# The experts' down products of a mixture-of-experts layer, all in passes of split operands, and their eviction on one engine

## The reference

```
for c in range(N_EXPERTS // EXPERT_CHUNK):
    g = einsum('td,edf->tef', xt, w_gate[sl])     # d = 1024, f = 256
    u = einsum('td,edf->tef', xt, w_up[sl])
    hdn = silu(g) * u * combine[:, sl, None]
    y = y + einsum('tef,efd->td', hdn, w_down[sl])
```

## Time and profile before

| | |
|---|---|
| median of 3 runs | 1458.14 us (1452.44 to 1460.0) |
| the profiled execution's own time | 1457.38 us |
| its span, first to last instruction | 1455.5 us |
| TensorE's granted clock, mean over the span; in the loop | 0.978; 1.00 |
| busy share of TensorE, VectorE, ScalarE, GpSimd | 94%, 68%, 47%, 31% |
| the loop over experts | about 785 to 1429 us |
| scatter `acc_dram<-arena` on the chain that ended last | 37% of the span |

### The profile page before, as it was taken

One profiled execution on the slowest core, in us unless ns is written; L12 is line 12 of the kernel. 1 busy time (PEld: TensorE's weight loads), 2 busy tenths in 40 slices (PEclk: granted clock), 3 DMA queues, 4 the chain that ended last, 5 costly groups with the idle time before them and its releaser, 6 DMA issues.

```text
span 1455.5 us, 19599 instructions
## 1 busy us (share of the span) xinstructions
PE 1372.3 (94%) x6615; PEld 983.9 (68%) x6615; DVE 988.4 (68%) x1415; ACT 687.0 (47%) x990; POOL 457.8 (31%) x384
## 2 busy tenths in 40 slices
PE   6989898999799999999999999999999999999990
PEld 5867677676688888885545666666666666666660
DVE  7997968785611111557635888888788888878765
ACT  4234554547422222310023766666666766766640
POOL 0422524333544444100010343332333322323322
PEclk8999999999999999999999999999999999999995
DMA  9044252535233333643057999999999999999954
GB/s 255 1 131 74 73 73 74 80 65 102 60 109 100 94 93 103 256 176 126 1 190 309 323 371 355 368 361 367 368 372 370 370 367 372 369 363 369 370 168 130
DMA packets 140775, 315.82 MB, mean 217 GB/s; under 512 B 18112, under 2 KB 99696, under 8 KB 115312
## 3 DMA queue, kind: packets, MB, share of 16 engines
q1 hardware_dynamic: 126384, 281.50, 55.6%
q0 software_dynamic: 14336, 33.59, 9.7%
HBM read 297.27 MB, written 34.54 MB: 228 GB/s over the span
## 4 chain that ended last, share of the span: by engine, by line
DMA 38%; PE 32%; DVE 12%; issue 8%; DVEq 4%; POOL 3%; POOLq 2%; ACT 1%
DMA acc_dram<-arena 37%; PE bank L728 8%; PE bank L730 8%; PE bank L729 8%; DVE arena L1418 6%; DVEq L1415 4%; PE bank L964 2%; PE bank L984 1%; DVE arena L1421 1%; POOL arena L675 1%; DVE arena L1696 1%; POOLq L634 1%; POOL arena L635 1%; PE bank L1058 1%; PE bank L735 1%
## 5 line engine op out<-in xcount | busy, mean ns | idle before, releaser
L1418 DVE TENSOR_TENSOR gate_up_low<-gate_up,gate_up_high 128x1024 fp32r<-128x1024 f32 x256 | 296.5, 1221 | 46.8 <-ACT gate_up_high L1164 46.3
L1164 ACT ACTIVATE arena<-bank 96x512 f32<-96x512 f32 (+5 forms) x244 | 128.8, 552 | 328.9 <-PE bank L730 129.0
L1164 ACT ACTIVATE gate_up_high<-gate_up 128x1024 fp32r<-128x1024 f32 x256 | 249.4, 1051 | 17.6 <-DMA gate_up<-moe_w_up_in 17.6
L1418 DVE TENSOR_TENSOR arena<-arena 128x512 f32<-128x512 f32 (+12 forms) x296 | 218.6, 771 | 16.9 <-ACT arena L1164 3.2
L728 PE MATMUL bank<-gate_up_high,rows_high 128*96 128x512 f32 x512 | 206.0, 402 | 4.4 <-DVE rows_low L1418 4.2
L730 PE MATMUL bank<-gate_up_high,rows_low 128*96 128x512 f32 x512 | 202.6, 396 | 0.0
L729 PE MATMUL bank<-gate_up_low,rows_high 128*96 128x512 f32 x512 | 200.9, 392 | 0.0
L735 PEld LDWEIGHTS bank<-arena 96*128 96x128 f32 (+5 forms) x1001 | 126.9, 187 | 54.4 <-issue 37.6
L595 POOL TENSOR_TENSOR wb_low<-arena,wb_high 128x1024 fp32r<-128x1024 f32 (+1 forms) x40 | 110.1, 2754 | 144.5 <-ACT wb_high L1164 144.5
L735 PE MATMUL bank<-arena 96*128 96x96 f32 (+5 forms) x1001 | 126.9, 265 | 8.5 <-DMA arena<-x_in 4.7
L1099 PE MATMUL bank<-down,arena 128*96 128x512 f32 x256 | 130.6, 592 | 0.0
(11 more groups left out here) (173 smaller groups left out, 2653.3 us busy)
## 6 DMA issues: line engine op xcount, KB each, us to landing
gate_up<-moe_w_gate_in SPq DMA_DIRECT2D x64, 1024.0 KB
gate_up<-moe_w_up_in SPq DMA_DIRECT2D x64, 1024.0 KB
down<-moe_w_down_in SPq DMA_DIRECT2D x64, 1024.0 KB
arena<-w_in_in SPq DMA_DIRECT2D x40, 512.0 KB, 4.1
arena<-w_glu_in SPq DMA_DIRECT2D x16, 512.0 KB, 4.0
arena<-w_lru_out_in SPq DMA_DIRECT2D x8, 768.0 KB, 4.7
arena<-x_in SPq DMA_DIRECT2D x8, 512.0 KB, 5.1
wu<-w_in_in SPq DMA_DIRECT2D x8, 512.0 KB, 6.6
```

The source lines that it names most:

```text
L1164: return nc.scalar.activation(out_, in_, func, **kw)
L1418: return V_.tensor_tensor(out_, a, b_, op)
```

## The change

Both halves of the down contraction are split: `down_high` and `down_low` are two operations each, `hid_high` and `hid_low` take both halves of hidden in one operation each, and `down` is 12 passes without a plain float32 matmul. ScalarE evicts both output halves, one after the other; VectorE's `y_kept` and its copy of the second half of hidden are gone, and so is the semaphore `y_e_dve`. The high parts of the down weights are now two buffers of twice the size, both on the shared expert's rows, so that expert 0's `down_high` waits for the stores.

```
-        heT = [at(b1 + 10240 + 512 * n, SL) for n in range(2)]
-        heT_hi = [part(f"hidden_high{n}", b1 + 10336 + 512 * n, 1, SL)[:, 0] for n in range(2)]
-        heT_lo = [part(f"hidden_low{n}", b1 + 10432 + 512 * n, 1, SL)[:, 0] for n in range(2)]
-        dn_hi = [part(f"down_high{n}", o, 1, D)[:, 0] for n, o in enumerate((sg_off + 4 * D, m_off))]
-        dn_lo = [part(f"down_low{n}", o, 1, D)[:, 0] for n, o in enumerate(dn_at)]
+        heT_hi = [part(f"hidden_high{n}", b1 + 10240 + 512 * n, 2, SL) for n in range(2)]
+        heT_lo = [part(f"hidden_low{n}", b1 + 10432 + 512 * n, 2, SL) for n in range(2)]
+        dn_hi = [part(f"down_high{n}", o, 2, D) for n, o in enumerate((m_off, m_off + 2 * D))]
+        dn_lo = [part(f"down_low{n}", o, 2, D) for n, o in enumerate(dn_at)]
...
             def add_expert(i, u):
                 pool.wait_ge(S["y_e_act"], 4 * i + u + 1)
-                pool.wait_ge(S["y_e_dve"], 4 * i + u + 1)
...
             def down(i, u):
                 pe.wait_ge(s_wdn[u % 4], 16 * i + 16 * (u // 4 + 1))
-                pe.wait_ge(S["dn_e_low"], 4 * i + u + 1)
+                pe.wait_ge(S["dn_e_low"], 8 * i + 2 * u + 2)
                 pe.wait_ge(S["hT_e_kept"], 4 * i + u + 1)
                 wait(pe, S["y_e_act"], 4 * i + u)
-                wait(pe, S["y_e_dve"], 4 * i + u)
                 for hf in range(2):
                     hs = slice(hf * 512, (hf + 1) * 512)
-                    mm3(banks[5 + hf][0:SL, :], heT_hi[u % 2], heT_lo[u % 2], dn_hi[u % 2][:, hs], dn_lo[u % 4][:, hs], True, False)
-                    last = mm(banks[5 + hf][0:SL, :], heT[u % 2], dn[u % 4][:, 1, hs], start=False, stop=True)
+                    for k in range(2):
+                        last = mm3(banks[5 + hf][0:SL, :], heT_hi[u % 2][:, k], heT_lo[u % 2][:, k],
+                                   dn_hi[u % 2][:, k, hs], dn_lo[u % 4][:, k, hs], k == 0, k == 1)
...
             def down_high(i, u):
                 act.wait_ge(s_wdn[u % 4], 16 * i + 16 * (u // 4 + 1))
                 wait(act, S["y_e_put"], 4 * i + u - 1)
-                if isinstance(i, int) and i == 0 and u == 1:
+                if isinstance(i, int) and i == 0 and u == 0:
                     act.wait_ge(S["acc_stored"], 16 * TT)
-                f(dn_hi[u % 2], dn[u % 4][:, 0], ACT.Copy).then_inc(S["dn_e_high"], 1)
+                for k in range(2):
+                    f(dn_hi[u % 2][:, k], dn[u % 4][:, k], ACT.Copy).then_inc(S["dn_e_high"], 1)

             def hid_high(i, u):
                 act.wait_ge(S["hT_e_put"], 4 * i + u + 1)
-                f(heT_hi[u % 2], banks[4][:, 0:SL], ACT.Copy).then_inc(S["hT_e_high"], 1)
+                f(heT_hi[u % 2], banks[4][:, 0:2 * SL].rearrange("p (k s) -> p k s", k=2), ACT.Copy).then_inc(S["hT_e_high"], 1)

             def y_kept(i, u):
                 wait(act, S["rows_added"], 64 * i + 16 * (u - 1))
                 act.wait_ge(S["y_e_put"], 4 * i + u + 1)
-                f(yb[u % 2][:, 0:512], banks[5][0:SL, :], ACT.Copy).then_inc(S["y_e_act"], 1)
+                f(yb[u % 2][:, 0:512], banks[5][0:SL, :], ACT.Copy)
+                f(yb[u % 2][:, 512:1024], banks[6][0:SL, :], ACT.Copy).then_inc(S["y_e_act"], 1)
...
-            def y_kept(i, u):
-                wait(dve, S["rows_added"], 64 * i + 16 * (u - 1))
-                dve.wait_ge(S["y_e_put"], 4 * i + u + 1)
-                V_.tensor_copy(yb[u % 2][:, 512:1024], banks[6][0:SL, :]).then_inc(S["y_e_dve"], 1)
...
-                dve.wait_ge(S["dn_e_high"], 4 * i + u + 1)
-                tt(dn_lo[u % 4], dn[u % 4][:, 0], dn_hi[u % 2].bitcast(f32), ALU.subtract).then_inc(S["dn_e_low"], 1)
-                if not isinstance(i, int) or u >= 1:
-                    y_kept(i, u - 1)
+                for k in range(2):
+                    dve.wait_ge(S["dn_e_high"], 8 * i + 2 * u + k + 1)
+                    tt(dn_lo[u % 4][:, k], dn[u % 4][:, k], dn_hi[u % 2][:, k].bitcast(f32), ALU.subtract).then_inc(S["dn_e_low"], 1)
                 wait(dve, S["y_e_put"], 4 * i + u - 1)
                 dve.wait_ge(S["hT_e_high"], 4 * i + u + 1)
-                V_.tensor_copy(heT[u % 2], banks[4][:, SL:2 * SL])
-                tt(heT_lo[u % 2], banks[4][:, 0:SL], heT_hi[u % 2].bitcast(f32), ALU.subtract).then_inc(S["hT_e_kept"], 1)
+                tt(heT_lo[u % 2], banks[4][:, 0:2 * SL].rearrange("p (k s) -> p k s", k=2), heT_hi[u % 2].bitcast(f32),
+                   ALU.subtract).then_inc(S["hT_e_kept"], 1)
```

More of the change, by code:

```diff
@@ L339, in decoder_layer @@
             sh_put sh_silu sh_hid sh_hT_put sh_hT sh_y_put sh_done texp_ready
-            xT_e_put xT_e_high xT_e_low g_e_put silu_e hid_e hT_e_put hT_e_kept y_e_put y_e_act y_e_dve
+            xT_e_put xT_e_high xT_e_low g_e_put silu_e hid_e hT_e_put hT_e_kept y_e_put y_e_act
              hT_e_high dn_e_high dn_e_low
@@ L1130, in _ @@
             pe.wait_ge(S["y_e_act"], E)
-            pe.wait_ge(S["y_e_dve"], E)
             pe.wait_ge(S["texp_ready"], 1)
@@ L2005, in _ @@
                 expert(0, n, more=n + 1 < E)
-            y_kept(0, E - 1)
             dve.wait_ge(S["rows_added"], 16 * E)
```

## The result

The changed kernel takes 1465.32 us (median of 7 runs, 1455.49 to 1473.51), against 1458.35 us for the kernel before (7 runs). The ratio of the means is 1.0066, 95% interval 1.004 to 1.0092: slower by 0.7% (the two medians lie 0.5% apart), where +0.2% was forecast and up to 1473 us was in the range. The same kernel, measured once more with the experiments, gives 1.0081 (1.0064 to 1.0099). The profiled execution has a span of 1465.9 us, 10.4 us more than before.

What follows compares the result with a forecast made beforehand. The prediction took the bytes of loads and scatters to set the late pace, with TensorE's gain waited away. Start +0.2 and index copy +3 on the profiled 1457.38 us gave 1460.6, rounded 1461; range 1450 to 1473.

Steps and rivals of the forecast that it cites:

- TensorE's 0.34 us: Down on TensorE: twelve split passes take 2.82 us, 0.34 less a stage, 9.40 instead of 9.74, all waited away again.
- Rival (1): In the expert loop TensorE is the bound and its gain arrives: 1436 us, or 1450 if only early stages keep it; chance 0.10.
- ScalarE and VectorE fit in: In each loop stage ScalarE's work rises to 8.4–8.7 us and VectorE's to 8.7, both below TensorE's 9.40.
- rival (3): The loop through ScalarE and VectorE becomes longer than the landings' period: 10.3 us a stage, +20, 1478 us; chance 0.08.
- the move of the phase: ScalarE's second eviction behind each landing moves the rest of the stage by 0.55 us; cost 0.
- The first down high part's wait for the stores: Before the loop, the shared expert's row stores land by 790.9, ahead of that part's start at 792.19; cost 0.
- ScalarE's wait for `acc_dram`: Sign in the profile after: ScalarE's wait for a landing, 127.5 us before, would be near half of that.
- The index copy: Between scatters, GpSimd's copy meets VectorE's second low part, ends 0.25 us later; after give-back 0.065 us a stage, +3 us.
- The gap of 1.3 us in that sum: Late stage of 9.956 us less a scatter's 8.6 us landing, used for the DMA rate of loads beside a scatter.
- Rival (2): GpSimd's copy waits 0.25 to 0.5 us in each of 59 stages, nothing given back: +15 to +30, 1473 us; chance 0.20.
- The tail: After the loads, scatters run serially, 6.0 us each; the later last eviction still leaves over 1 us; cost 0.
- the start: Start of the scatter chain: expert 0's evictions in a row, and the index copy meeting a low part, cost +0.2 us.

## Why the prediction held, and which of its terms were off

What bounds the kernel: right. Full DMA engines and the chain of scatters set the late stages; without the scatters TensorE does, and without half of TensorE's down work nothing is gained.

TensorE's 0.34 us: 9.40 us a stage was forecast and 9.41 measured, down 2.82 and 2.88. That it is waited away again was right, with ten fast stages instead of 22; the forecast was "ten or so". Rival (1) is refuted.

ScalarE and VectorE fit in: right. Their second low part, second high part and eviction leave TensorE's 9.41 us untouched in the kernel without scatters, so rival (3) is out, and the move of the phase (0.55 us forecast, 0.56 measured) costs nothing by itself. The first down high part's wait for the stores cost nothing: the first down load after TensorE's first result came at 802.18 instead of 802.90. One of the signs missed: ScalarE's wait for `acc_dram` fell from 127.5 to 102.3 us and not to half.

The index copy: the mechanism was right, and where the stages are steady its price was too. From the 11th to the 49th scatter the copies take 5.0 us more and the landings 2.4 less, which leaves 2.6 us in 38 stages, 0.07 each, where 0.065 was forecast. In the second measurement of the changed kernel it is 4.2 more and 2.3 less. The quicker landings are thus seen in the traces, though their size is only roughly known: these 38 stages take 377.7 to 379.6 us in the kernels whose late copies are short. (The gap of 1.3 us in that sum is 1.36 by its own numbers, which moves none of its results.) That a later landing meets less of the low part was foreseen; in half of the stages it meets none.

The loop still lost 8.2 us where 3 were forecast, and the step that came out too small is the sum itself: it took one steady stage for all. It left out the eight scatters from the 49th to the 57th, with 3.1 us. They take 83.9 to 84.9 us in all five traces that have the loss in the loop, and 81.0 to 82.1 in the five kernels without it that copy the index at the usual place. TensorE's pause and half clock fall among them in all five. They aren't the whole cause, since the changed kernel with VectorE's eviction has both and takes 81.4. The first ten intervals have another 2.4 us, with landings 3.9 us slower in all. But these ten differ by 2 us among the kernels without the loss, so this part isn't clear of noise.

Rival (2) has a part of the truth by its number: 1465 lies between the forecast of 1461 and its 1473. Its condition, low parts under every landing and nothing given back, isn't met: 26 of 58 copies took over 0.3 us, and the mean wait is 0.19 us against its 0.25 to 0.5. The prediction's own sign for it, late landings over 10.1 us apart, came up all the same. The down loads are 10.14 us apart after the first ten, and the scatters 10.16 from the 23rd on. That the time lies within the range is thus in part luck: it is at the upper edge of the forecast's own 1454 to 1465, and the range reached further up only for this rival.

The tail: cost 0 was forecast, on the ground that the last eviction leaves a microsecond. It looked at the last rows and not at GpSimd's own issue. The long issue costs about 4 us, of which the quicker landings after the loads hide a part: the profiled executions stand 7.8 us apart at the 59th scatter and 10.4 us at the end.

The sum of the measured terms, 8.2 - 0.4 for the start + 2.6, is the 10.4 us between the two spans. The forecast of 3.2 missed 5.2 of them in the loop and 2.6 in the tail, and had the start 0.6 too late.

What stays open: why landings are slower behind the 49th scatter, and what ties them to TensorE's pause. And the price of either loss differs from execution to execution by more than the two together explain: the changed kernel's times spread over 18 us.

## What to carry to other kernels

A chain of DMAs that each wait for the last one's landing is paid for in what lies between landing and next issue. Before you put work with two operands in SBUF on VectorE, see what GpSimd does at that moment. Take out of the gap what can be done ahead (here the index copy: 0.8 to 0.9% of the changed kernel, nothing of the kernel before). An edit that takes work from one of two bounds that lie 2% apart brings the second bound and whatever the moved work disturbs; the gain of 22 us was real and could be seen only when the scatters were gone.

## What the runs showed of the hardware that was not expected

What holds GpSimd up is a run of VectorE's operations with two operands in SBUF, and it can be held to the end of the whole run. A copy of 0.18 us took 4.58 us beside four such subtractions in a row and ended right behind the fourth, while VectorE went on without a gap. Most copies were let in behind one operation, though.

The issue of an indirect DMA took 8.78 us instead of 1.45 beside VectorE's nine microseconds of work, 5.79 in another kernel, and 3.97 with a pause made for it. In all three it ended 1.30 to 1.31 us behind the last subtraction with two operands in SBUF; the operations with one operand in PSUM that followed didn't hold it.

A semaphore that GpSimd raises in program order behind the issue of an indirect DMA comes up before that issue has ended by the profile, here 0.22 us ahead of its start (1406.33 and 1406.55).
